# Rotary row swaps as on-chip transfers instead of matmuls, keys first, and one query wait per pair of heads

## The reference

```
first block, per layer:
  qa, ka = grid_rope(rmsnorm(q)), grid_rope(rmsnorm(k))   # 8 query heads, 2 key heads, width 64
      x1, x2 = halves of 16 features;  out = [x1*cos - x2*sin, x2*cos + x1*sin]
  y_attn = softmax(qa ka^T / 8) v;   beside it a gated delta rule over the same projections
  x += out((gate_a * y_attn + gate_d * y_delta));  x += feed-forward(x)
second block, per layer:
  q (8 heads), k_s, k_w (2 heads each) are normed and turned by _rope: halves of 32 features
  x += branches of three attentions (NSA, forgetting, memory), merged by gates
```

## Time and profile before

| | |
|---|---|
| median of 3 runs | 3375.83 us (3370.58 to 3378.57) |
| the profiled execution | 3376.13 us, its span 3374.1 us |
| mean granted TensorE clock | 0.984 of full |
| PE busy | 3207.3 us (95%) |
| DVE, ACT, POOL busy | 1880.1, 1411.8, 430.3 us |
| transfers | 249.10 MB, 23.0% of 16 engines' time on SP's queue |

### The profile page before, as it was taken

The page is one execution under the profiler, slowest core; times in us unless marked ns, Lnnn a source line. Parts: engine busy times, 40 slices in busy tenths (PEclk is TensorE's granted clock), DMA queues, the critical chain, the costliest instruction groups (busy, mean ns, idle before and its releaser), DMA issues.

```text
span 3374.1 us, 60750 instructions
## 1 busy us (share of the span) xinstructions
PE 3207.3 (95%) x26204; PEld 2532.3 (75%) x26204; DVE 1880.1 (56%) x2890; ACT 1411.8 (42%) x2478; POOL 430.3 (13%) x444
## 2 busy tenths in 40 slices
PE   8798999999999889999999999999999999999999
PEld 5577777878876577778788876767788767676787
DVE  6476656666466565656756564553534554535443
ACT  5544223433245544333433344544433455544432
POOL 0042330000000140420000000120301001204010
PEclk9899999999999999999999999999999999999999
DMA  4001113332331001113233232212122222122222
GB/s 156 26 21 40 42 32 105 101 104 92 96 120 57 20 22 52 40 52 109 90 98 102 92 121 64 75 50 70 60 91 72 87 81 94 51 60 66 76 76 93
DMA packets 75210, 249.10 MB, mean 74 GB/s; under 512 B 9280, under 2 KB 10944, under 8 KB 73920
## 3 DMA queue, kind: packets, MB, share of 16 engines
q1 hardware_dynamic: 74944, 245.22, 23.0%
HBM read 237.88 MB, written 6.29 MB: 72 GB/s over the span
## 4 chain that ended last, share of the span: by engine, by line
PE 81%; DVE 8%; ACT 5%; POOL 3%; issue 2%; DMA 0%; SPq 0%; POOLq 0%; ACTq 0%; DVEq 0%
PE psum L518 78%; PE psum L700 2%; POOL s_xb L2672 2%; DVE s_xb L1961 2%; DVE s_tmp L1964 1%; ACT s_tmp L1255 1%; DVE s_ffy L1964 1%; DVE s_w L1961 1%; POOL s_tmp L2672 1%; ACT s_w L1255 1%; ACT s_E L1255 1%; DVE s_nm L2045 1%; ACT L1255 0%; PE psum L605 0%; ACT L1267 0%
## 5 line engine op out<-in xcount | busy, mean ns | idle before, releaser
L518 PE MATMUL psum<-s_h,s_w 128*128 128x512 f32 (+1 forms) x6864 | 1667.0, 400 | 29.7 <-DVE s_tmp L1964 18.0
L518 PEld LDWEIGHTS psum<-s_h,s_w 128*128 128x128 f32 (+1 forms) x6864 | 1289.0, 190 | 338.6 <-issue 47.9
L1961 DVE TENSOR_TENSOR s_w<-s_stage,s_w 128x1024 fp32r<-128x1024 f32 (+2 forms) x468 | 529.0, 1131 | 426.2 <-ACT s_w L1255 424.5
L1255 ACT ACTIVATE s_w<-s_stage 128x1024 fp32r<-128x1024 f32 (+2 forms) x468 | 451.6, 966 | 304.2 <-PE psum L518 282.0
L518 PE MATMUL psum<-s_ffa,s_w 128*128 128x512 f32 x1056 | 242.1, 390 | 4.6 <-DVE s_ffa L1961 4.6
L518 PEld LDWEIGHTS psum<-s_ffa,s_w 128*128 128x128 f32 x1056 | 197.8, 188 | 48.0 <-DVE s_ffa L1961 7.1
L518 PE MATMUL psum<-s_oR,s_w 128*128 128x512 f32 (+1 forms) x960 | 214.6, 375 | 0.0
L2704 POOL TENSOR_SCALAR s_E<-s_E,s_inv,s_g 128x128 f32<-128x128 f32 (+3 forms) x128 | 76.6, 608 | 1076.1 <-DVE s_inv L2065 1054.9
L2672 POOL TENSOR_TENSOR s_xb<-s_xb,s_cstm 64x512 f32<-64x512 f32 x64 | 92.5, 1446 | 932.8 <-DVE s_xb L1961 928.4
L2045 DVE TENSOR_REDUCE s_nm<-psum 128x1 f32<-128x512 f32 (+3 forms) x288 | 137.5, 519 | 99.2 <-PE psum L518 98.6
L1964 DVE SCALAR_TENSOR_TENSOR s_ffy<-psum,s_pcol,s_ffy 128x511 f32<-128x511 f32 x176 | 131.7, 748 | 108.6 <-ACT s_ffy L1255 105.5
(11 more groups left out here) (284 smaller groups left out, 3667.6 us busy)
## 6 DMA issues: line engine op xcount, KB each, us to landing
s_stage<-w SPq DMA_DIRECT2D x192, 512.0 KB, 3.5
s_stage<-wup SPq DMA_DIRECT2D x88, 512.0 KB, 3.5
s_stage<-wo SPq DMA_DIRECT2D x32, 512.0 KB, 3.4
s_stage<-wdn SPq DMA_DIRECT2D x32, 512.0 KB, 3.5
s_stage<-wdn SPq DMA_DIRECT2D x16, 384.0 KB, 3.0
spill<-s_x SPq DMA_DIRECT2D x2, 2048.0 KB, 9.1
s_stage<-woa SPq DMA_DIRECT2D x16, 256.0 KB, 2.7
s_x<-spill SPq DMA_DIRECT2D x2, 2048.0 KB, 8.0
```

The source lines that it names most:

```text
L518: return self.e.matmul(out, left, right, start=first, stop=last, skip_group_check=True)
L1255: return self.e.activation(out, src, func, **kw)
L1961: return self.e.tensor_tensor(out, a, b, op)
```

## The change

- PE's `qk` does the sum only. The permutation `K_PA` and the bank `b2` are gone; `K_PB` stays, unsigned, for `hidden`. The sign moves into the sine tables.
- SP swaps the rows: new `turn(turned, span, before)` waits for `xg` and starts 128/span transfers of span partitions by 2 KB from `xg` to another on-chip buffer: 8 of 32 KB in the first block (span 16), 4 of 64 KB in the second (span 32). The buffers are `early2` (first block) and `U[0..3]` (second; from the fifth on SP first waits for the buffer's last reader).
- DVE's `qk` waits for the transfers in place of the matmul and writes t1 in place.
- SP runs `ahead(key, 4)` and `turn` for each tile in turn; weight tiles further on, and in the second block the memory input and the compression weights, come behind it in SP's order.
- First block: the order is keys, q0, q1, q2, q3 (`ORDER_Q = (4, 0, 1, 2, 3)`). The scores wait for the keys and, by `each`, for their own pair's queries; the wait for the values moves from `score` to `pv`.
- The first table load is 4 tiles of 64 KB, not 5.

```diff
+ORDER_Q = (4, 0, 1, 2, 3)
+    for which, span in enumerate(SPANS):
+        ropes[:, 2 * which + 1] *= np.where(p % (2 * span) < span, f32(-1), f32(1))
@@ Program
+    def turning(self, l):
+        m = self.m
+        if isinstance(l, tuple):
+            keys = [(l, "q", c) for c in range(4)] + [(l, "k", b) for b in range(2)]
+            return [(key, n, m.U[:, n % 4, :]) for n, key in enumerate(keys)]
+        return [((l, "q", c), c, m.early2[:, c, :]) for c in ORDER_Q]
@@ grid_attn
-                [("vec_qk", (l, "q", 4), "out"), ("act_attn", l, "v")], 0, 0, clear=[("dma_spill", l)], lag=1)
+                [("vec_qk", (l, "q", 4), "out")], 0, 0, each=lambda p: ("vec_qk", (l, "q", p), "out"), clear=[("dma_spill", l)], lag=1)
@@ Tensor.qk
-        if perm is not None:
-            b2 = self.take((key, "b2"))
-            self.w.wait_ge(*self.at("act_qk", key, "xg"))
-            self.mm(b2[:, 0:n], self.const(perm), self.tmp((key, "xg"))[:, 0:n], True, True).then_inc(*self.up("pe_sum", key, "swap"))
-            self.give((key, "b2"), ("vec_qk", key, "t1"))
@@ score
+            if f.each is not None:
+                self.after([f.each(p)])
@@ pv
+            if tag[0] == "A":
+                self.w.wait_ge(*self.at("act_attn", tag[1], "v"))
@@ Vector.qk
-            self.w.wait_ge(*self.at("pe_sum", key, "swap"))
-            self.tt(u, self.bank((key, "b2"))[:, 0:n], m.rope[:, 1, 0:n], ALU.mult).then_inc(*self.up("vec_qk", key, "t1"))
+            self.w.wait_ge(*self.at(f"dma_turn{n1}", key, 128))
+            self.tt(u, u, m.rope[:, 1, :], ALU.mult).then_inc(*self.up("vec_qk", key, "t1"))
@@ Sync
+    def turn(self, turned, span, before):
+        key, n, to = turned
+        xg = self.tmp((key, "xg"))
+        self.w.wait_ge(*self.at("act_qk", key, "xg"))
+        if before is not None:
+            self.w.wait_ge(*self.at("vec_qk", before, "out"))
+        for i in range(0, 128, 2 * span):
+            for a, b in ((i, i + span), (i + span, i)):
+                self.e.dma_start(to[a:a + span, :], xg[b:b + span, :]).then_inc(*self.landed(f"dma_turn{n}", key, a + span))
@@ Sync.layer1
+        for turned in self.turning(l):
+            self.ahead(turned[0], 4)
+            self.turn(turned, SPANS[0], None)
@@ Sync.layer2
-                self.ahead((L, "q", 3))
-                self.w.wait_ge(*self.prod((L, "q", 3)))
-                ...
+                for n, turned in enumerate(self.turning(L)):
+                    self.ahead(turned[0], 4)
+                    self.turn(turned, SPANS[1], self.turning(L)[n - 4][0] if n >= 4 else None)
+                    if n == 3:
+                        ...
```

More of the change, by code:

```diff
@@ L30 @@
 C2_N = 88
-K_ID, K_ONE, K_BO, K_PA, K_PB, K_TU, K_TL = range(7)
-K_EA = 7
-K_N1 = 11
+K_ID, K_ONE, K_BO, K_PB, K_TU, K_TL = range(6)
+K_N0, K_EA = 4, 6
+K_N1 = 10
+SPANS = 16, 32
 M_TU, M_TL = range(2)
@@ L50, in constants @@
     z[:, K_BO] = same
-    for which, span in ((K_PA, 16), (K_PB, 32)):
-        lo = (n % (2 * span)) < span
-        z[:, which] = np.where(lo, -1.0 * (p == n + span), 1.0 * (p == n - span))
+    z[:, K_PB] = p == np.where(n % 64 < 32, n + 32, n - 32)
     z[:, K_TU] = same & (p <= n)
@@ L462, with __init__ @@
 class Attn:
-    def __init__(self, q, k, v, klen, causal, row, E, PT, made, base, tile, dv=64, clear=(), lag=2):
+    def __init__(self, q, k, v, klen, causal, row, E, PT, made, base, tile, dv=64, clear=(), each=None, lag=2):
         self.q, self.k, self.v, self.klen, self.causal, self.row = q, k, v, klen, causal, row
-        self.clear = clear
+        self.clear, self.each = clear, each
         self.E, self.PT, self.made, self.base, self.tile, self.dv = E, PT, made, base, tile, dv
@@ L779, in rest @@
             if c < 5:
-                self.qk((l, "q", c), K_BO, K_PA)
+                self.qk((l, "q", ORDER_Q[c]), K_BO)
             elif c == 5:
@@ L1108, in layer2 @@
         for _ in behind(lambda c: self.lin(two(c), wt[l, 14 + c], 8, hi, lo, ht) if c < 8 else next(values),
-                        lambda c: self.qk(two(c), K_BO, None) if c < 8 else None, 9):
+                        lambda c: self.qk(two(c), K_BO) if c < 8 else None, 9):
             pass
@@ L1460, in layer1 @@
         self.w.wait_ge(*self.at("dma_par", l, "row"))
-        self.ahead((l, "q", 0))
+        self.ahead((l, "q", ORDER_Q[0]))
         tag = ("mix", l) if l else "in"
@@ L1473, in first @@
             if 0 < c < 6:
-                self.qk_begin(keys[c - 1], self.at("vec_scaled", keys[c - 1]), C1["qn"] if c < 5 else C1["kn"])
+                self.qk_begin(keys[c - 1], self.at("vec_scaled", keys[c - 1]), C1["kn"] if c == 1 else C1["qn"])
                 next(uppers, None)
@@ L1487, in layer1 @@
         scalars, begun = self.scalars(l), self.project(l, 0, (0,))
-        keys = [(l, "q", c) for c in range(5)] + [(l, "v"), (l, "bd"), (l, "p", 0, 0, 0)]
+        keys = [(l, "q", c) for c in ORDER_Q] + [(l, "v"), (l, "bd"), (l, "p", 0, 0, 0)]
         for _ in behind(first, rest, 8, LAG):
@@ L2013, in normal, with qk @@
         return self.norm(tag, [self.m.x[:, c, :] for c in range(8)], lambda c: self.at(*made(c)), col, *self.m.mixh)
-    def qk(self, key, dst, scale, perm, n=T):
+    def qk(self, key, dst, scale, turned, n=T):
         m = self.m
         xg, s = self.tmp((key, "xg"))[:, 0:n], self.tmp((key, "s"))[:, 0:n]
-        if perm:
-            u = self.take((key, "u"))[:, 0:n]
-            self.w.wait_ge(*self.at("pe_sum", key, "swap"))
-            self.tt(u, self.bank((key, "b2"))[:, 0:n], m.rope[:, 1, 0:n], ALU.mult).then_inc(*self.up("vec_qk", key, "t1"))
-            self.tt(xg, xg, m.rope[:, 0, 0:n], ALU.mult).then_inc(*self.up("vec_qk", key, "t2"))
+        if turned is not None:
+            _, n1, u = turned
+            self.w.wait_ge(*self.at(f"dma_turn{n1}", key, 128))
+            self.tt(u, u, m.rope[:, 1, :], ALU.mult).then_inc(*self.up("vec_qk", key, "t1"))
+            self.tt(xg, xg, m.rope[:, 0, :], ALU.mult).then_inc(*self.up("vec_qk", key, "t2"))
             self.w.wait_ge(*self.at("vec_qk", key, "t2"))
@@ L2120, in rest @@
             if c < 5:
-                self.qk((l, "q", c), m.aq[:, c, :] if c < 4 else m.ak[:, :], 0.125 if c < 4 else 1.0, True)
+                self.qk(keys[c], m.aq[:, c - 1, :] if c else m.ak[:, :], 0.125 if c else 1.0, self.turning(l)[c])
             elif c == 6:
@@ L2435, in rest @@
             if c < 4:
-                self.qk(keys[c], m.bq[:, c, :], 0.125, True)
+                self.qk(keys[c], m.bq[:, c, :], 0.125, self.turning(L)[c])
             elif c in (4, 6):
-                self.qk(keys[c], m.bk[:, c // 2 - 2, :], 1.0, True)
+                self.qk(keys[c], m.bk[:, c // 2 - 2, :], 1.0, self.turning(L)[c // 2 + 2])
             if 5 <= c < 7:
@@ L2478, in layer2 @@
         for _ in behind(lambda c: self.ahead((L, "mq", c) if c < 4 else (L, "mg", 1, 0)),
-                        lambda c: self.qk((L, "mq", c), m.bq[:, c, :], 128.0 ** -0.5, False) if c < 4 else next(fill), 5):
+                        lambda c: self.qk((L, "mq", c), m.bq[:, c, :], 128.0 ** -0.5, None) if c < 4 else next(fill), 5):
             pass
@@ L2788, in run @@
                 self.one_ahead()
-        self.e.dma_start(m.cst[:, :, :], d["cst1"][:, 0:5, :]).then_inc(*self.landed("dma_cst"))
+        self.e.dma_start(m.cst[:, :, :], d["cst1"][:, 0:K_N0, :]).then_inc(*self.landed("dma_cst"))
         self.e.dma_start(m.valid[:, :], d["cvalid"]).then_inc(*self.landed("dma_valid"))
```

35 lines of the change are left out of this document (17 added, 18 removed).

## The result

The kernel after takes 3362.9 us (median of 10 runs, 3360.1 to 3371.0) where the kernel before, beside it, takes 3375.8 (10 runs, 3369.4 to 3378.6). The ratio is 0.9968, with an interval of 0.9960 to 0.9976: 11 us faster by the ratio, 13 by the medians. Forecast were 20 us and 3356, in a range of 3348 to 3367. So the sign and the range held, and a third to a half of the expected gain is missing.

A forecast was written before the change was run, and what follows sets the result against it. TensorE, with 81% of the chain, was taken as the bound. Two layers at 5.8 us and two at 4.3 gave 20.2 us off 3376.1, so 3356 (68%), with an 80% range of 3348 to 3367.

The forecast's parts named there:

- A swap costs PE 0.86 us: Query phases: each of 22 swaps taken from PE saves 7.21 - 6.35 = 0.86 us, 18.9 us if PE is the bound.
- First block, 5.8 us a layer: Front of grid attention: fewer swaps and no wait before the first score; ACT decides the gain, bounds 4.3 and 7.4.
- ACT meeting row: First block, where ACT makes a weight tile's high part after waiting for PE: from 83.52 to about 77.7.
- Second block, 4.3 us a layer: Five swaps ahead of v0's transposes go, so ACT's run starts 4.3 us earlier; 5.2 or 3.6 as bounds.
- PE's wait at the memory squares: Second block: the sixth swap's removal only lengthens this wait, from 3.01 to 3.9 us.
- SP has the time and its lateness is hidden: SP's queue: 0.5 us a start, 4.0 or 2.0 us a tile; weight tiles 1 to 1.3 us late, mostly covered.
- Transfers hidden, no DVE wait: First block: turned rows land 6.2 to maybe 10 us after `xg`; about 12 us are there before DVE wants them.
- The other edits at nothing: t1 from on-chip memory, the values' wait moved to `pv`, and later compression weights were each costed at nothing.
- SP can't keep up: Rival: at 1.39 us a start, 11.1 us a tile, first-block turns land 22.7 us late a layer; 3401, 5%.
- All pays: Rival: the clock and the wait pay in full, 2 x 7.4 + 2 x 5.2 = 25.2 us; 3351, 14%.
- Block 1 pays nothing: Rival: DVE and ACT work that doesn't move sets grid attention's front, only the second block pays; 3367.5, 9%.
- Nothing moves: Rival: the PE time that goes comes back as waits for late weights in four places; 3375, 4%.

The follow-up runs named there:

- e1: Kernel after, with SP issuing the weight tile five beyond the turned one before the turn, in both blocks; 3352.0 us, ratio 0.9938.
- e4: Kernel after, with all 128 transfers issued from GpSimd and SP's weight tiles back in their old places; 3356.9 us, ratio 0.9950.
- e7: Kernel of e1 with the old order: queries first, keys last, all pairs waiting for keys and values; 3357.7 us, ratio 0.9953.
- e8: Kernel after, with the weight tile issued before the turn in block 1 alone; 3358.2 us, ratio 0.9964.
- e11: Kernel of e1 run again, on one chip with e9 and e10; 3355.4 us, ratio 0.9946.
- e5: Kernel after, with block 1's tiles moved in 4 transfers of 32 rows, not 8 of 16 (rows misplaced, only times used); 3358.6 us, ratio 0.9960.
- e6: Kernel of e1 with each block 1 transfer cut into two of 8 rows, 16 starts a tile; 3400.1 us, ratio 1.0084.
- e2: Kernel before with only the keys-first order and narrower waits, swaps still on PE and no transfers; 3373.8 us, ratio 1.0001.
- e3: Kernel after with the old order: queries first, keys last, all pairs waiting for keys and values; 3367.4 us, ratio 0.9983.
- e9: Kernel after, unchanged, run again on one chip with e10 and e11; 3366.6 us, ratio 0.9976.
- e10: Kernel after, with the weight tile issued before the turn in block 2 alone; 3363.4 us, ratio 0.9970.

## Why the prediction was right and wrong

- **A swap costs PE 0.86 us: right.** The step is 6.34 us (37.12 to 43.46), where a swap was in it 7.2.
- **First block, 5.8 us a layer: right in mechanism, and in size once SP is out of the way.** With the tile first (e1, e4, e7, e8, e11) it is 5.9 us in both layers by the second table. In e1 the ACT meeting row is at 76.82 (forecast: 77.7). In the kernel after the first score came at 65.30 (forecast: 65), but the meeting row is at 83.58, and of the 11.6 us for two layers it got 4.7 in both executions.
- **Second block, 4.3 us a layer: right with e1's edit**, 4.36 us in each layer of each such execution. PE's wait at the memory squares is 3.4 us, forecast 3.9. As changed, it lost more than the 0.7 us a layer that I had as the lower bound: PE waited 1.2 to 2.0 us for weights in layer 0 and 0.8 to 1.3 in layer 1.
- **SP has the time and its lateness is hidden: this step failed.** The forecast had the tile behind the first turn 1 us late, covered by PE's lead, and put it at nothing in the sum. It cost 6 us in block 1, layer 0, and 10 to 13 us in the four layers. It had three errors. A start takes 0.62 us and not 0.50, and the first turn 6.19 us and not 4.0 (in block 1, layer 0, the first turn takes 5.4 to 6.3 us in every run with eight starts on SP, in layer 1 it takes 4.95; why isn't shown). The tile landed 4.3 us after its start and not 3.5. So it was 3.96 us late, not 1. And the cover was read on the wrong engine: PE indeed never waited for these weights (its step stayed at 6.34), but the end of this stretch is set by ACT and DVE, as I had written myself for the meeting row. Both take their work in order, so what stood behind the late high and low parts on them, the last head's turn and the convolution, moved with them: the convolution by 6.3 us (e1), the sum of the two waits. That the time still fell into the range is owed in part to luck: the range was that wide for the scatter and, in part, for the case that block 1 gains nothing; for late weights it had 0.7 us a layer of block 2.
- **Transfers hidden, no DVE wait: right.** The rule of the Trainium skill that I had weighed against the change ("DMA: Bandwidth & Descriptors", "Rules for kernel authors": coalesce small transfers) pointed at the term that failed, though the time that I had given it (3401) didn't come. e5 and e6 agree with it: 4, 8 and 16 starts a tile take 2.4, 4.9 and 10.7 us.
- **The other edits at nothing: right.** The compression weights made no engine late (in the kernel after they go at 2049.33, and the next high parts wait for nothing); the memory input did, by ACT's 4.66 and 6.54 us, which its idle time covered. t1 takes 0.68 us from on-chip memory and took 0.69 from psum. The order and the narrower wait, for which I had 1.5 us a layer in the term of block 1, bring 1.2 alone by the second table (e2, nothing that its timed runs can tell) and nothing beside transfers with the tile first (e7).
- **Rivals.** "SP can't keep up" is real from 10.7 us a tile (e6); at 4.9 it is not. "All pays" (3351) is the time that e1 reaches, but not its mechanism: the stretches gave 20.6 us, as forecast, and not 25.2. "Block 1 pays nothing" holds for its layer 0 in the kernel after, through late weights and not through work that doesn't move: e1 moved the row behind the wait of 4.09 us too, from 96.68 to 89.92. "Nothing moves" had the cause that took the missing part, PE time that comes back through late weights, and a size that didn't come.

The version that beats both kernels is e1: 3352.0 and 3355.4 us in its two sets of runs, 0.9938 and 0.9946 of before.

## What to carry to other kernels

When small transfers are put on a queue that also prefetches, count starts and not bytes, and look at the first prefetch behind each of them; issue the prefetch whose buffer is free before the waiting transfer. Test the cover of a late tile on the engine that sets the end of the stretch, with all that stands behind the tile in that engine's order, not on the engine that consumes it. A queue of an idle engine did the same here without any order to find (e4: the stretches of e1, timed 0.9950 and 0.9938).

## What the runs showed of the hardware

A wait of PE costs more than itself only in some cases. Windows of the kernel after and of e8 behind their waits for weights (from:to, us; busy PE, PEld, DVE, ACT, POOL; granted clock; DMA share; GB/s):

```profile
2023.40:2030.00 6.60, 6.52 (x26) 4.80 (x26) 5.73 (x10) 5.66 (x9) 0.00 (x0) 1.00 0.39 93
```

```profile
2018.20:2025.00 6.80, 6.77 (x23) 5.43 (x24) 5.92 (x10) 5.66 (x9) 0.00 (x0) 0.75 0.40 98
```

Behind the wait of 1.23 us the same 24 matmuls take 5.78 us at the full 2.4 GHz, behind 2.53 us 7.32 us, part of them at 1.2 GHz: 1.5 us more. Behind 1.48 us (e3) they take 5.78, behind 2.02 us (e9) 7.35. The length of the wait doesn't settle it by itself: at the memory squares PE waits 3.38 us in the kernel after and 3.39 in e1, and the four records behind take 1.13 us (2060.13 above) and 2.08:

```profile
2045.53 2.08 PE L528 MATMUL psum<-s_tmp,s_cst 128*128 128x256 f32 x4 [3.39 <-ACT s_tmp L1264]
```

The scatter of this kernel, 11 us between its fastest and its slowest run, is partly clock in stretches that no experiment touches. Windows of e1 and of e10 in the second block's attention, the code and the work being the same (e10 is 9.9 us later there):

```profile
2180.00:2220.00 40.00, 35.60 (x248) 25.75 (x247) 22.32 (x62) 18.64 (x60) 8.88 (x18) 1.00 0.23 67
```

```profile
2190.00:2230.00 40.00, 37.63 (x221) 27.31 (x221) 19.39 (x52) 16.29 (x51) 6.81 (x14) 0.83 0.24 66
```

From 2072.83 to 2674.79 of the kernel before e1 needs 0.1 us more than it, e10 6.0. So a difference of less than 6 us between two profiled executions of this kernel must be placed in a stretch before it is believed, and intervals of timed runs decide.
